# Feed-forward by seven products of quarter blocks instead of eight, with u in device memory and the down products kept in PSUM

## What is computed

```python
x = x + _rms(jnp.einsum('btc,cd->btd', mix, P['w_out']), P['norm_mix_post'])
h2 = _rms(x, P['norm_ffn_pre'])
u = jnp.square(jax.nn.relu(jnp.einsum('btd,df->btf', h2, P['w_up'])))
x = x + _rms(jnp.einsum('btf,fd->btd', u, P['w_down']), P['norm_ffn_post'])
```

## Time and profile before

| | us |
|---|---|
| median of 3 timed runs (lowest, highest) | 2010.35 (2009.53, 2010.56) |
| span of the profiled execution | 2008.4 |
| TensorE busy in it | 1819.3 (91%) |
| VectorE, ScalarE, GpSimd busy | 821.1, 614.2, 396.8 |
| first feed-forward matmul, from the span's start | 1230.75 |
| bytes moved by DMA | 100.07 MB |

### The profile page before, as it was taken

The page is one execution under the profiler, slowest core; times in us unless marked ns, Lnnn a source line. Parts: engine busy times, 40 slices in busy tenths (PEclk is TensorE's granted clock), DMA queues, the critical chain, the costliest instruction groups (busy, mean ns, idle before and its releaser), DMA issues.

```text
span 2008.4 us, 33890 instructions
## 1 busy us (share of the span) xinstructions
PE 1819.3 (91%) x13839; PEld 1519.3 (76%) x13839; DVE 821.1 (41%) x1320; ACT 614.2 (31%) x1421; POOL 396.8 (20%) x606
## 2 busy tenths in 40 slices
PE   4999999999775798788887996999999999999996
PEld 4999999844454666388873445999999999999995
DVE  7111111166337764734321454344444444433336
ACT  3111111266355554523321222222222222222223
POOL 6400021288335454320010001000000000000004
PEclk9999999999887755689978997999999999999998
DMA  5211131200461111000004101111111111121102
GB/s 150 59 42 34 42 95 56 72 26 1 125 179 41 32 27 29 12 2 2 2 1 156 34 26 53 42 42 42 42 51 54 42 42 42 43 58 45 42 21 89
DMA packets 103829, 100.07 MB, mean 50 GB/s; under 512 B 15522, under 2 KB 89906, under 8 KB 103714
## 3 DMA queue, kind: packets, MB, share of 16 engines
q1 hardware_dynamic: 91266, 81.15, 13.8%
q0 software_dynamic: 6720, 17.11, 2.9%
q10 hardware_dynamic: 5728, 0.19, 0.2%
HBM read 85.78 MB, written 12.65 MB: 49 GB/s over the span
## 4 chain that ended last, share of the span: by engine, by line
PE 51%; DVE 4%; ACT 1%; DMA 1%; issue 1%; POOLq 0%; POOL 0%; SPq 0%; DVEq 0%
PE ps L416 12%; PE ps L418 12%; PE ps L417 12%; PE ps L2422 6%; PE ps L2063 1%; PE ps L2084 1%; PE ps L2080 1%; PE ps L1987 1%; DVE arena L2596 1%; DMA arena<-in_w_out 1%; PE ps L2515 1%; PE ps L2514 1%; PE ps L2136 0%; DVE arena L2173 0%; PE ps L2134 0%
## 5 line engine op out<-in xcount | busy, mean ns | idle before, releaser
L416 PE MATMUL ps<-h_split,w_split 128*128 128x384 f32 (+1 forms) x768 | 251.1, 327 | 3.4 <-DVE w_split L2577 3.4
L418 PE MATMUL ps<-h_split,w_split 128*128 128x384 f32 (+1 forms) x768 | 250.9, 327 | 0.0
L417 PE MATMUL ps<-h_split,w_split 128*128 128x384 f32 (+1 forms) x768 | 250.8, 327 | 0.0
L2607 DVE TENSOR_TENSOR arena<-arena,ps 128x1024 f32<-128x1024 f32 x144 | 175.6, 1220 | 148.7 <-PE ps L418 139.8
L418 PE MATMUL ps<-w_split,u_split 128*128 128x512 f32 x512 | 199.4, 389 | 0.0
L417 PE MATMUL ps<-w_split,u_split 128*128 128x512 f32 x512 | 199.3, 389 | 0.0
L416 PE MATMUL ps<-w_split,u_split 128*128 128x512 f32 x512 | 199.2, 389 | 0.0
L2637 POOL TENSOR_TENSOR arena<-arena 128x1024 f32<-128x1024 f32 (+1 forms) x9 | 22.3, 2482 | 760.1 <-DVE arena L2596 760.1
L2585 DVE TENSOR_TENSOR u_split<-above_u_split,u_split 128x384 fp32r<-128x384 f32 (+1 forms) x96 | 49.4, 515 | 295.9 <-ACT above_u_split L2558 295.8
L2537 ACT ACTIVATE w_split<-below_w_split 128x1024 fp32r<-128x1024 f32 x64 | 64.1, 1048 | 325.0 <-PE ps L418 307.5
L416 PEld LDWEIGHTS ps<-h_split,w_split 128*128 128x128 f32 x768 | 144.7, 188 | 4.2 <-issue 3.6
(11 more groups left out here) (389 smaller groups left out, 3622.5 us busy)
## 6 DMA issues: line engine op xcount, KB each, us to landing
below_w_split<-in_w_up SPq DMA_DIRECT2D x32, 512.0 KB, 5.0
below_w_split<-in_w_down SPq DMA_DIRECT2D x32, 512.0 KB, 4.0
w_raw<-in_w_in SPq DMA_DIRECT2D x27, 512.0 KB, 4.0
arena<-in_x_prompt SPq DMA_DIRECT2D x16, 512.0 KB, 3.7
arena<-in_cache_sb_k SPq DMA_DIRECT2D x64, 128.0 KB, 2.8
arena<-in_cache_sb_v POOLq DMA_DIRECT2D x64, 128.0 KB, 2.9
nat_scratch<-nat_stage POOLq DMA_DIRECT2D x32, 128.0 KB, 2.0
arena<-nat_scratch SPq DMA_DIRECT2D x16, 256.0 KB, 2.8
```

What stands on the lines that cost most here:

```text
L416: pe.matmul(out, w_hi, x_hi, start=first, stop=False)
L417: pe.matmul(out, w_hi, x_lo, start=False, stop=False)
L418: return pe.matmul(out, w_lo, x_hi, start=False, stop=last)
L2607: dve.tensor_tensor(y, y, p, ALU.add).then_inc(S("dn_out"), 1)
```

## The change

Both projections are computed by the Winograd form of Strassen's scheme on 2 x 2 blocks: seven products of quarter blocks and sums of blocks before and after.

Up: 16 chunks again, each with block row `A1*`/`A2*` (128 hidden columns of the lower and of the upper half) and the features in two halves; tokens 0 to 511 and 512 to 1023 are the two token halves. The token side is summed once, into seven forms `T1` to `T4`, `T_B22`, `T_B21`, `T_B11` with hi and lo, kept in SBUF. The weight side is summed for each chunk by VectorE (`sum_form`: `S1` to `S4`). A product is 4 x 3 matmuls of 512 columns; "snapshots" of the partial sums in PSUM are copied by ScalarE (`take`), and `corner` adds them on VectorE. The samples are not in the scheme: `samples` runs 2 x 8 x 3 matmuls of 64 columns a chunk. u goes to `u_scratch` in device memory (4 x 256 KB a chunk), the sample part stays in SBUF. `x1` goes to `x1_scratch` and is read again at the end.

Down: the seven products run one after the other over all 16 chunks and stay in PSUM: `M24` and `M53` are two products each that share their loads (32 steps each), `M1`, `M6` and `M7` one each (16 steps each), 112 steps in all. A step is 4 token tiles x 3 matmuls of 512 columns. For each step VectorE makes one sum (`down_sum`), ScalarE the hi parts of both sides (`down_high`), VectorE the lo parts (`down_low`); three sets of these are kept. The raw blocks come by `down_load` in units: of four DMAs of 256 KB for two steps in `M24` and `M53`, of two such DMAs for one step in the others (`NIN` = 3 semaphores). At the end of a product ScalarE and VectorE bring its four PSUM banks into y (`copied`, `corners`). The samples add two matmuls of 512 columns for each of 64 blocks, beside `M1` (two a step), `M6` and `M7` (one a step). `y_acc` and its zeroing are gone; GpSimd adds nothing any more; the output projection's transposes of tile i-1 stand at three quarters of tile i.

```diff
-        def mlp_tensor(pe):
...
-            def accumulate(n, tiles):
...
-            pool.memset(y_acc, 0.0).then_inc(S("dn_out"), 1)
...
+        UP_ORDER = (("P1", "P2", "P5", "P6", "P7", "P4", "P3", "smp"),
+                    ("P1", "P2", "P6", "P5", "P7", "smp", "P4", "P3"))
...
+            def product(c, bank, weight, tokens, first):
+                for k in range(4):
+                    out = ps[:, bank, :]
+                    w_hi, w_lo = sf[weight][:, 0, k, :], sf[weight][:, 1, k, :]
+                    x_hi, x_lo = fm[tokens][0][:, k, :], fm[tokens][1][:, k, :]
+                    pe.matmul(out, w_hi, x_hi, start=(first and k == 0), stop=False, skip_group_check=True)
+                    pe.matmul(out, w_hi, x_lo, start=False, stop=False, skip_group_check=True)
+                    ins = pe.matmul(out, w_lo, x_hi, start=False, stop=(k == 3), skip_group_check=True)
+                ins.then_inc(S("up_ps"), 1)
+            def samples(c, bank):
+                for ft in range(2):
+                    out = ps[:, bank, ft * SMP:(ft + 1) * SMP]
+                    for k in range(KD):
+                        form = ((A11, A12), (A21, A22))[ft][k // 4]
+                        w_hi, w_lo = sf[form][:, 0, k % 4, :], sf[form][:, 1, k % 4, :]
+                        pe.matmul(out, w_hi, hs[:, 0, k, :], start=(k == 0), stop=False, skip_group_check=True)
+                        pe.matmul(out, w_hi, hs[:, 1, k, :], start=False, stop=False, skip_group_check=True)
+                        ins = pe.matmul(out, w_lo, hs[:, 0, k, :], start=False, stop=(k == KD - 1),
+                                        skip_group_check=True)
+                ins.then_inc(S("up_ps"), 1)
...
+        STEPS = ([(s, j, y) for s in ("M24", "M53") for j in range(NCH) for y in range(2)]
+                 + [(s, j, 0) for s in ("M1", "M6", "M7") for j in range(NCH)])
+        UNITS = [(s, j) for s in ("M24", "M53", "M1", "M6", "M7") for j in range(NCH)]
+        UNIT_BLOCKS = {"M24": (B11, B21), "M53": (B22, B12, None), "M1": (B11, B22), "M6": (B11, B12), "M7": (B21, B22)}
+        UNIT_A = {"M24": (("A21", A21_0), ("A22", A22_0)), "M53": (("A11", A11_0),), "M1": (), "M6": (), "M7": ()}
...
+        def down_load(sp, u):
+            s, j = UNITS[u]
+            done = S(f"q_in{u % NIN}")
+            if u >= NIN:
+                sp.wait_ge(*upto("q_lo", unit_steps(u - NIN)[-1] + 2))
+            small = [m for m, (v, b) in enumerate(SMALL) if v <= u - NIN]
+            if small:
+                sp.wait_ge(*upto("z_lo", small[-1] + 1))
...
+            w = A["w_down"][0].rearrange("(n p) c -> n p c", p=P)
+            for b in UNIT_BLOCKS[s]:
+                if b is None:
+                    sp.dma_start(block_at(u, b), u_dram[NCH + j, :, 0:512]).then_inc(done, 16)
+                else:
+                    sp.dma_start(block_at(u, b), w[NCH * (b // 2) + j, :, 512 * (b % 2):512 * (b % 2) + 512])\
+                        .then_inc(done, 16)
+            for name, base in UNIT_A[s]:
+                ft, half = {"A21": (0, 1), "A22": (1, 1), "A11": (0, 0)}[name]
+                sp.dma_start(a_tile(base, j), u_dram[NCH * ft + j, :, 512 * half:512 * half + 512]).then_inc(done, 16)
...
+        def slot_free(eng, n):
+            if n >= 3:
+                eng.wait_ge(*upto("q_ps", step_done(n - 3)))
+            else:
+                eng.wait_ge(*upto("up_ps", up_done(NCH - 1, "smp")))
...
+        def down_sum(dve, step, n):
+            s, j, y = STEPS[n]
+            u = unit_of(n)
+            unit_loaded(dve, u)
+            slot_free(dve, n)
+            a11, a21, a22 = a_tile(A11_0, j), a_tile(A21_0, j), a_tile(A22_0, j)
...
+            else:
+                b, d = UNIT_BLOCKS[s]
+                ins = dve.tensor_tensor(df_sum(n, 1), block_at(u, b), block_at(u, d), ALU.add)
+            ins.then_inc(S("q_sum"), 1)
+        def down_high(act, n):
+            act.wait_ge(*upto("q_sum", n + 1))
+            for side, src in enumerate(sides(n)):
+                ins = act.activation(df[n % 3][side][:, 0, :], src, ACT.Copy)
+            ins.then_inc(S("q_hi"), 1)
+        def down_low(dve, step, n):
+            s, j, y = STEPS[n]
+            dve.wait_ge(*upto("q_hi", n + 1))
+            for side, src in enumerate(sides(n)):
+                ins = dve.tensor_tensor(df[n % 3][side][:, 1, :], src, df[n % 3][side][:, 0, :].bitcast(F32),
+                                        ALU.subtract)
+            ins.then_inc(S("q_lo"), 1)
+            if s == "M53" and y == 1:
+                a11, a21, a22 = a_tile(A11_0, j), a_tile(A21_0, j), a_tile(A22_0, j)
+                dve.tensor_tensor(a21, a21, a11, ALU.subtract).then_inc(*did("dve"))
+                dve.wait_ge(*upto("q_lo", n + 1))
+                dve.wait_ge(*so_far("dve"))
+                step(dve.tensor_tensor(a11, a11, a22, ALU.add))
+                dve.tensor_tensor(a22, block_at(unit_of(n), None), a22, ALU.subtract).then_inc(*did("dve"))
...
+            for n, (s, j, y) in enumerate(STEPS):
+                for m in small_before(n):
+                    small(m)
+                pe.wait_ge(*upto("q_lo", n + 1))
+                for t in range(4):
+                    if j == 0:
+                        bank_free((s, y), t)
+                    out = ps[:, BANKS[s, y][t], :]
+                    a_hi, a_lo = (df[n % 3][0][:, z, t * P:(t + 1) * P] for z in range(2))
+                    b_hi, b_lo = (df[n % 3][1][:, z, :] for z in range(2))
+                    pe.matmul(out, a_hi, b_hi, start=(j == 0), stop=False, skip_group_check=True)
+                    pe.matmul(out, a_hi, b_lo, start=False, stop=False, skip_group_check=True)
+                    ins = pe.matmul(out, a_lo, b_hi, start=False, stop=(j == NCH - 1), skip_group_check=True)
...
+                ins.then_inc(S("q_ps"), 1)
+                for m in small_after(n):
+                    small(m)
...
+            AFTER = {32: (), 33: (("M24", 1),), 64: (("M53", 0),), 65: (("M53", 1),), 81: (("M1", 0),),
+                     97: (("M6", 0),)}
+            down_sum(dve, step, 2)
+            for n in range(2, len(STEPS)):
+                s, j, y = STEPS[n]
+                if n + 1 < len(STEPS) and n not in AFTER:
+                    down_sum(dve, step, n + 1)
+                down_low(dve, step, n)
+                for product in AFTER.get(n, ()):
+                    dve.wait_ge(*so_far("dve"))
+                    for t in range(4):
+                        corners(*product, t)
+                for m in small_of(n):
+                    small_low(dve, m)
+                if n in AFTER and n + 1 < len(STEPS):
+                    down_sum(dve, step, n + 1)
...
```

More of the change, by code:

```diff
@@ L2325, in build @@
[L2325 to L2328 removed]
+        CA = (MIXER_CONSTS + P + 7) // 8 * 8
+        F0 = CONST_END
+        assert F0 % 8 == 0 and PR == F0 + KD * TOK
+        FEND = F0 + 7 * 4096
+        HRAW = FEND + 1024
+        SF = HRAW + 8192
+        RAW0 = SF + 8192
+        NCH = 16
+        W_LOADS = [len(range(g, len(W_UNITS), RSLOTS)) + len(range(g, LT, LA_RING)) for g in range(RSLOTS)]
+        w_out = at(PR, KD, D)
+        h2 = at(PR + KD * D, 2, D)
@@ new lines, in out_vector @@
+        def out_vector(dve):
+            step = chain(dve, "dve")
+            for i in range(NT - 1):
+                out_residual(dve, step, i)
+                if i >= 1:
+                    out_evac(dve, step, i - 1)
+                out_norm(dve, i)
+                if i == 3:
+                    for form in SUMS:
+                        sum_form(dve, step, 0, form)
+                if i == 4:
+                    for form in range(8):
+                        low_form(dve, 0, form)
+            out_evac(dve, step, NT - 2)
@@ new lines, in up_sync, with store @@
+        def up_sync(sp):
+            def store(c, name):
+                ft, half = {"C11": (0, 0), "C12": (0, 1), "C21": (1, 0), "C22": (1, 1)}[name]
+                sp.wait_ge(*upto("u_sq", u_done(c, name)))
+                sp.dma_start(u_dram[NCH * ft + c, :, 512 * half:512 * half + 512], u_block(c, name))\
+                    .then_inc(S(f"u_out{c % 2}"), 16)
+            for name in ("C22", "C11", "C21"):
+                store(0, name)
+            sp.wait_ge(*upto("t_lo", 5))
+            load_up(sp, 2)
+            for c in range(1, NCH):
+                store(c - 1, "C12")
+                if c + 2 < NCH:
+                    sp.wait_ge(*upto("up_lo", 8 * c + S4 + 1))
+                    load_up(sp, c + 2)
+                if c == NCH - 1:
+                    for u in range(2):
+                        down_load(sp, u)
+                for name in ("C11", "C22", "C21"):
+                    store(c, name)
+            down_load(sp, 2)
+            store(NCH - 1, "C12")
@@ new lines, in small_of, with small_before, small_after @@
+        def small_of(n):
+            return [m for m, (v, b) in enumerate(SMALL) if v == unit_of(n)]
+        def small_before(n):
```

(26 more changed lines are left out.)

950 lines of the change are left out of this document (676 added, 274 removed).

## The result

The changed kernel takes 2167.9 us (median of 4 runs, 2161.7 to 2177.6) against 2010.5 us before (median of 4). The ratio is 1.078, with a 95% interval of 1.075 to 1.082. The direction was forecast, the size was not: 2087 us were predicted, and the range ended at 2130.

The account below looks back on a forecast made before the run. TensorE's matmul spacing bound the kernel before; afterwards load chains bind M1, M6, M7. Up ends at 1608.8, M24 1696.1, M53 1799.3, the rest 2068.9, tail 2084.7, plus 1.95 outside: 2087 us (3.8% slower), range 2030 to 2130.

Parts of the forecast that it names:

- The front: Before the up stage: without memset and its cast, the first product starts at 1211.2 us, 19.5 earlier.
- Chunk 0: First chunk of the up stage: waits for the token forms and snapshots make it 32.0 us against 24.4 of matmuls.
- Chunks 1 to 15: Rest of the up stage: 24.37 us a chunk, sample matmuls 0.111 us each, no holes; up ends at 1608.8.
- rival 4: M1, M6, M7: the clock falls in TensorE's gaps; at 1.2 GHz steps of 7.25 and 6.35 us, 2140 us; 8%.
- Rival 2: Up stage: the sample matmuls hide their weight loads, 54 us less, 2032 us; 12%.
- M24 and M53: First down products: M24 is TensorE's with loads hidden, 87.3 us; M53 is VectorE's, 6.26 us a pair, 103.2 us.
- one chain for all 48 single steps: M1, M6, M7: low part, SyncE's wait, two DMAs, landing, sum, next low in line; 5.55 us a step.
- small lows (0.88 or 1.76 us) lie inside it: M1, M6, M7: VectorE's low parts for the samples are hidden in the load's wait, adding nothing to a step.
- 3.5 us of wait: M1, M6, M7: VectorE waits 3.5 us a step for the load, from issue to landing; bounds 3.3 to 4.3.
- Rival 1: M1, M6, M7: the load chain does not bind; 163.0 us in place of 247.9, 2002 us in total; 7%.

Follow-up runs that it names:

- groups of twelve: Against the changed kernel: the 48 sample matmuls of a chunk in four groups of 12, each behind a wide product, instead of one run; 2124.1 us.
- woven: Against the changed kernel: in chunks 1 to 15 the 48 sample matmuls stand one behind each 512-column matmul of four products; 2141.1 us.
- the order turned: Against the changed kernel: M1's two small sample products run ahead of the next step instead of behind it; 2127.4 us.
- The load experiment: Against the changed kernel: SyncE loads a unit of M1, M6 or M7 one step sooner; 2125.8 us.
- the two edits together: Against the changed kernel: M1's small sample products ahead of the next step, and down loads one step sooner; 2033.5 us.
- The wide form: Against the changed kernel: samples' high and low parts side by side, 128 columns under the high weights, 32 matmuls a chunk in one run; 2103.3 us.

## Why the prediction was wrong

**The front.** Right in its working. The memset and its cast are gone, and VectorE's last sum of tile 7 and the first product stand where the working put them:

```profile
1217.54 0.69 DVE L2635 TENSOR_TENSOR arena<-arena 128x512 f32<-128x512 f32 x1
1217.94 0.19 PEld L2675 LDWEIGHTS ps<-h_form,up_form 128*128 128x128 f32 x1 [0.81 <-issue]
```

The 6.7 us by which this is later than 1211.2 arose ahead of the changed code: the first `w_out` load was issued at 1078.34, against 1071.76 before. In the seven experiments, whose code is the same up to there, the first product starts between 1207.4 and 1215.4. So this is the spread between runs, not the change.

**Chunk 0.** 35.1 us in place of 32.0. The gaps were forecast and had the full clock; that it is 0.50 in the samples behind them, from 1244.4 us on, was not.

**Chunks 1 to 15: a step that failed.** The distance of 0.111 us and the 24.4 us chunk were right, and so were the holes, "which I have at none after chunk 0". What failed is the silent step from "TensorE never waits" to "the clock stays full". It put the cost of the clock at nothing without a row for such a run; it measured 35.7 us in chunks 1 to 15 of this trace, nearly half the miss. In groups of twelve 31 of them came back. The Trainium skill ("TensorE: Matmul & The Clock Gate", section "HAM oscillation — how this bites in real kernels") describes the clock falling over waits for a DMA. I applied it where there are waits (rival 4) and nowhere else. The window above shows a fall with TensorE busy throughout, so the section's case is not the only one.

**Rival 2** (samples hide their weights) was wrong, and my rejection of it right: a sample matmul cost 0.111 us in runs and groups and 0.12 woven, and with 128 columns no more than with 64. Of the Trainium skill's section "Back-to-back issue gap" (same page), the part I cited excludes weight loads and would have given 66 us less. The same section also says that in a stream of loads and matmuls both set the spacing. That holds here: with the same weights the distance is 0.111 us at 64 and at 128 columns and 0.227 at 512. Its figure for 128 columns, 81 ns, doesn't: this case measured 0.111 us.

**M24 and M53.** Right: 87.2 against 87.3, and 100.1 against 103.2. The start of M53 cost 9.3 us for two steps where 10.1 was worked out.

**M1: the step that failed most.** The prediction priced one chain for all 48 single steps. It even had the second in its sum, as "small lows (0.88 or 1.76 us) lie inside it", without asking what the small lows wait for. They wait for ScalarE, ScalarE for a small slot, and the slot for a product that TensorE runs only behind the next step. With three slots and two small products a step, that is a wait of one whole step of TensorE. It made the step 8.6 us in place of 5.55, 40 us over steps 66 to 79. With the order turned the step was 5.63. The half clock of 1.2 GHz that rival 4 spoke of occurred here in part (0.79). It came with the pauses of the slot chain and not of the chain of loads, but as TensorE's step is a link of the slot chain it counted there: some 23 of the 40 us, by the estimate above. In M6 and M7, where the pauses are those that rival 4 meant, the clock was 0.90, and the steps were no longer than forecast.

**M6 and M7: the step "3.5 us of wait" was right.** The mean step from 82 to 111 was 5.35 us against 5.47 worked out with the passage between the products; a plain step took some 5.2 in place of 5.55, and a few took up to 7.8. The load experiment settles the cause: one earlier request, and VectorE's wait went from 60.2 to 10.7 us.

**Rival 1** (no load chain, 2002 us) was rightly given little. It also priced what the two edits together would give: with both chains open the kernel took 2033.5 us. In the profiled run the down stage began 36 us late, 30 of them from chunks 1 to 15 and 4 from chunk 0. Behind that, the stretch from M53 to step 66 was 7 us shorter than in its sum and steps 66 to 111 were 7 us longer, so that the rest of its sum comes out partly by luck.

The range was too narrow because all its rivals varied terms that were already in the sum. None stood for a chain not seen, or for a clock below full in the stage with the most TensorE work.

## What to carry to other kernels

When a step has several queues handing slots round, write out the chain for every slot, the small ones too: for each instruction that waits for a slot, ask which instruction frees it and what stands ahead of that one on its engine. A wait that hides something (small lows, the finish of a tile) is cover; shorten it, and what lay beneath it is the next bound, so of two chains on one step each alone shows only a part of what both give. Don't put many matmuls with few columns in one run (here 48 of 64 columns cost 31 us of a stage of 401), even where TensorE never waits; spread them over the wide ones, behind a product whose evacuation needs the cover, and give each weight load as many columns as there are.

## What the runs showed of the hardware

- The granted clock fell from 1.00 to 0.50 in a run of 48 matmuls of 64 columns, 0.111 us apart, without a pause of TensorE, in 11 of the 14 chunks from 2 to 15; in three further kernels with the same run, in 11, 14 and 10. The wide form, 32 matmuls in 3.6 us, lost it in 3 of 14. Groups of 12 matmuls (1.33 us) between wide products did not lose it in any.
- Float32r matmuls with full 128x128 weights stand 0.111 us apart with 64 columns (a pair of 128 and 64 columns takes 0.22) and 0.227 with 512. Matmuls of 64 columns with 64x64 weights, in plain float32, start 0.058 us apart (median of one line in a mixer).
- Loads of 256 KB landed in 2.8 us (median) in M6 and M7 at 137 GB/s, and in 3.0 us at 192 GB/s.
- At the half clock the distances grew to 0.213 us for 64 columns and 0.427 for 512.
